# Memory cross-attention: the order of scores, transposes and value products against the query chunks

## The chip, the cores and the metric

One NeuronCore of a Trainium2 chip runs the whole program. The metric is the time of one execution on the device in microseconds; it is given as a median of several runs. All times below that have a place ("at 1289.87") are microseconds from the first instruction of one profiled execution. In the rows of the windows each busy time is followed by its instructions in brackets, and a clock of 1.00 is the full 2.4 GHz.

## The reference, cut to what matters

The program computes a long chain of layers on 256 tokens of width 1024: a gated linear attention, a differential attention, two MLPs, a mixing block with a convolution, a state-space branch and a sliding-window attention, then a cross-attention to a memory of 256 entries, and a last MLP. The change touches the cross-attention only:

```python
def memory_cross_attention(h, mem_h, w_q, w_kv, q_g, k_g, w_o):
    q = rms_norm_2((h @ w_q).reshape(b, l, XATTN_HEADS, XATTN_HEAD_DIM), q_g)   # 4 heads of 256
    kv = mem_h @ w_kv
    k = rms_norm_2(kv[..., :D_MODEL].reshape(b, m, XATTN_HEADS, XATTN_HEAD_DIM), k_g)
    v = kv[..., D_MODEL:].reshape(b, m, XATTN_HEADS, XATTN_HEAD_DIM)
    logits = jnp.einsum("bqhd,bkhd->bhqk", q, k).astype(jnp.float32) * (XATTN_HEAD_DIM ** -0.5)
    probs = jax.nn.softmax(logits, axis=-1)
    out = jnp.einsum("bhqk,bkhd->bqhd", probs.astype(v.dtype), v).reshape(b, l, D_MODEL)
    return out @ w_o
```

`h` is the residual stream after the mixing block. All of it is fp32.

## The kernel before, in words

**Chunks.** All large weights are one stream of 420 chunks of 1024 x 128, numbered in the order in which they are used. The mix output is chunks C_MIX = 332 to 339, the query projection C_XQ = 340 to 347, the attention's output projection C_XO = 348 to 355, the last MLP starts at C_M2 = 356. SyncE loads two chunks at a time (a slab, 1 MB) into a ring of four (`raw`). ScalarE (ACT) copies a chunk to an fp32r high part `w_hi` (`cut_hi`, line 1064), VectorE (DVE) subtracts and writes the bf16 rest `w_lo` (`cut_lo`, line 1692). Both run three chunks ahead (AHEAD = 3) in four slots. TensorE (PE) multiplies a chunk in 24 matmuls: 16 with `w_hi` against the high and low part of the activations (lines 425 and 426), 8 with `w_lo` (line 435). The result, 128 x 256, lies in one PSUM bank until DVE reads it out, which is called eviction here and counted by the semaphore `bank_free`. Chunks go round four banks, 0 to 3; `chunk(..., banks=2)` goes round banks 0 and 1 and waits before its first matmul for the eviction of the chunk two before it. The activations come in three forms, too (`operand` on ACT makes the high and the bf16 form, `operand_lo` on DVE the low one), and the first chunk of a group waits for them one by one.

**Order.** There is no scheduler: each engine has its own instruction order, written out by hand, and semaphores between them. An instruction that waits holds up all behind it on its engine.

**The stage of the change.** On PE the eight query chunks come first. Behind chunk 0 is a matmul for the row norm (`stats(6)`, its logarithm and exponential on ACT are `rms(6)`), and DVE needs that to evict chunk 0 (`scaled`, line 1711, multiplies by it). Two chunks are one head of the query. When both are evicted, ACT squares them (`pair_sq`, line 1543), PE sums the squares with a matmul of ones (`pair_sums`, line 923), ACT makes the reciprocal root in two steps (`pair_rstd`, lines 1547 and 1550), and DVE multiplies the head by gain and root (`pair_out`, line 2224). The pair sums 4 to 7 of the query use banks 4 and 5 in turn (`pair_sums_at`).

Then, after all chunks, come the four heads of attention, all in plain fp32 matmuls, which the trace shows as two instructions each:

- `x_scores(h)` on PE, line 1010, eight instructions, into bank 4 + h%2. The scores of head h + 1 stand before the transposes of head h. The first waits until all queries are normed.
- maximum on DVE (`x_max`, line 2318), exponential with sums on ACT (`x_exp`, line 1651), reciprocal and weights on DVE (lines 2332, 2334).
- transposes on PE (line 1023), into bank 6; copy to SBUF on ACT (line 1662).
- value products on PE (line 1032), eight instructions, into bank 7 or 3.
- ACT reads them into the operand of the output projection (`operand`, lines 1070, 1071: four casts a head), DVE makes the low part (`x_lo`, line 1705). The output chunks' first one waits for these one by one, so its last products wait for head 3.

Of the kernel before, what the change touches and what calls it, by code (L numbers as in the profile page):

```python
# [24 lines left out]
T = 256  # L25
KC = D // P
# [11 lines left out]
X_HEADS = 4  # L38
# [37 lines left out]
AHEAD = 3  # L76
# [14 lines left out]
OUT_BANKS = (7, 3)  # L91
# [26 lines left out]
def program(nc, w_d, par_d, con_d, gm_d, x_d, mem_d, band_d, out_d):  # L118
    ctx = ExitStack()
    with ctx:  # L120
# [159 lines left out]
        x_q = cut(KC, T)  # L280
# [81 lines left out]

        def pair_sums_at(k):

            return ps[:, 2 if k < X_HEADS else 4 + k % 2, 0:T]

        def tap_sums(i):

# [39 lines left out]
        def _(pe):  # L408
            mm = nc.tensor.matmul

            def chunk(c, j, X, build, banks=BANKS):

                chunk_hi(c, j, X, build, banks)
                chunk_rest(c, j, X, build, banks)
# [88 lines left out]
            def chunks(c0, n, X, build, banks=BANKS):  # L503
                for j in range(n):
                    chunk(c0 + j, c0 + j, X, build if j == 0 else None, banks)

            def stats(nu, row, tok):

                pe.wait_ge(sq_step, (2 * KC - 1) * (nu + 1))
                if nu:  # L510
                    pe.wait_ge(rstd_done, nu)
                if row:
                    last = mm(stat_rstd(), ones[:], sumsq[:], start=True, stop=True)
                if tok:
                    for t in range(NT):
                        last = mm(stat_tok()[:, t:t + 1], sumsq[:, t * P:(t + 1) * P], ones[:, 0:1], start=True, stop=True)
                last.then_inc(stat_mm, 1)
# [398 lines left out]
            def pair_sums(k):  # L916
                pe.wait_ge(xa["sq"], k + 1)
                if k >= 2:
                    pe.wait_ge(xa["r"], k - 1)
                if 0 < k < X_HEADS:  # L920
                    pe.wait_ge(xa["r"], k)
                for i in range(2):
                    last = mm(pair_sums_at(k), ones[:], x_sq[:, k % 2, i], start=i == 0, stop=i == 1)  # L923
                last.then_inc(xa["mm"], 1)
# [67 lines left out]
            chunks(C_MIX, 8, XB, XB_MIX)  # L992


            for n in range(9):
                if n < 8:
                    chunk(C_XQ + n, C_XQ + n, XA, XA_XQ if n == 0 else None)
                    if n == 0:
                        stats(6, True, False)
                if n and n % 2 == 0:  # L1000
                    pair_sums(4 + n // 2 - 1)

            def x_scores(h):
                if h == 0:
                    pe.wait_ge(xa["out"], 16)
                if h >= 2:
                    pe.wait_ge(xa["p"], h - 1)
                for t in range(NT):
                    for i in range(2):
                        last = mm(ps[:, 4 + h % 2, t * T:(t + 1) * T], x_q[:, 2 * h + i, t * P:(t + 1) * P], x_k[:, 2 * h + i],  # L1010
                                  start=i == 0, stop=i == 1)
                last.then_inc(xa["s"], 1)

            x_scores(0)
            for h in range(X_HEADS):
                if h + 1 < X_HEADS:
                    x_scores(h + 1)
                pe.wait_ge(xa["n"], h + 1)
                if h:
                    pe.wait_ge(xa["pt"], h)  # L1020
                for k in range(2):
                    for t in range(NT):
                        last = nc.tensor.transpose(ps[:, 6, k * T + t * P:k * T + (t + 1) * P], x_p[:, h % 2, t, k * P:(k + 1) * P], ident)
                last.then_inc(xa["t"], 1)
                pe.wait_ge(xa["pt"], h + 1)
                if h >= 2:
                    pe.wait_ge(XB.lo_done, KC * XB_XO + 2 * h - 2)
                    pe.wait_ge(XB.bf_done, KC * XB_XO + 2 * h - 2)
                for half in range(2):
                    f = slice(h * T + half * P, h * T + (half + 1) * P)  # L1030
                    for k in range(2):
                        last = mm(ps[:, OUT_BANKS[h % 2], half * T:(half + 1) * T], x_v[:, k, f], x_pt[:, h % 2, k], start=k == 0, stop=k == 1)  # L1032
                last.then_inc(xa["o"], 1)
            chunks(C_XO, 8, XB, XB_XO)
            mlp(C_M2, 2, XA_MLP2, C_M2 - 3, 0, XB_MLP2, 7)

# [2 lines left out]
        def _(act):  # L1039
# [13 lines left out]
            def cut_hi(c, j):  # L1053

                if isinstance(c, int) and c >= CHUNKS:
                    return
                if j % 2 == 0:
                    if isinstance(c, int):
                        act.wait_ge(slab_in[j // 2 % RING], 16 * (c // 2 // RING + 1))
                    else:  # L1060
                        act.wait_ge(slab_in[j // 2 % RING], 2 * (c - j % 8) + 16)
                if not isinstance(c, int) or c >= HI_SLOTS:
                    act.wait_ge(gemm_done, c - HI_SLOTS + 1)
                nc.scalar.copy(w_hi[:, j % HI_SLOTS].rearrange("p k n -> p (k n)"),  # L1064
                               raw[:, j // 2 % RING, j % 2]).then_inc(hi_done, 1)
# [10 lines left out]
            def rms(nu, to, to_tok=None):  # L1076

                act.wait_ge(stat_mm, nu + 1)
                if to_tok is not None:
                    A(lnt_tok[:], stat_tok(), ACT.Ln, bias=eps[:, 0:1], scale=1.0 / D)  # L1080
                done(A(lnt[:, 0], stat_rstd(), ACT.Ln, bias=eps[:, 0:1], scale=1.0 / D))
                if to_tok is not None:
                    A(to_tok[:], lnt_tok[:], ACT.Exp, scale=-0.5)
                A(to[:], lnt[:, 0], ACT.Exp, scale=-0.5).then_inc(rstd_done, 1)
# [546 lines left out]
                operand(XB, XB_MIX, n, merged[:, n])  # L1631
            residual(C_MIX, XA, XA_XQ, "norm_xattn")

            cut_hi(C_XQ + AHEAD, C_XQ + AHEAD)
            for n in range(10):
                if n < 8:
                    if n < 7:
                        cut_hi(C_XQ + n + 1 + AHEAD, C_XQ + n + 1 + AHEAD)
                    if n == 0:
                        rms(6, rstd)  # L1640
                    if n % 2:
                        pair_sq(4 + n // 2, C_XQ + n, x_q[:, n - 1:n + 1])
                if n >= 2 and n % 2 == 0:
                    pair_rstd(4 + n // 2 - 1)

            def x_exp(h):
                act.wait_ge(xa["max"], h + 1)
# [4 lines left out]
                            accum_out=x_st[:, h % 2, 2 + t:3 + t])  # L1652
                ins.then_inc(xa["p"], 1)

            x_exp(0)
            for h in range(X_HEADS):
                if h + 1 < X_HEADS:
                    x_exp(h + 1)
                act.wait_ge(xa["t"], h + 1)
                if h >= 2:  # L1660
                    act.wait_ge(xa["o"], h - 1)
                nc.scalar.copy(x_pt[:, h % 2].rearrange("p a b -> p (a b)"), ps[:, 6, :]).then_inc(xa["pt"], 1)
                act.wait_ge(xa["o"], h + 1)
                for half in range(2):
                    operand(XB, XB_XO, 2 * h + half, ps[:, OUT_BANKS[h % 2], half * T:(half + 1) * T])
            residual(C_XO, XA, XA_MLP2, "norm_mlp2")
            mlp(C_M2, 2, 7, 0, None, None, None)

# [7 lines left out]
        def _(dve):  # L1676
# [32 lines left out]
            def scaled(c, j, to, banks=BANKS):  # L1709

                TT(to, got(c, j, banks), rstd[:], ALU.mult).then_inc(bank_free, 1)
# [590 lines left out]
            residual(C_MIX, XA, XA_XQ, "norm_xattn")  # L2302


            for n in range(12):
                if n < 8:
                    c = C_XQ + n
                    cut_lo(c + AHEAD, c + AHEAD)
                    if n == 0:
                        dve.wait_ge(rstd_done, 7)  # L2310
                    scaled(c, c, x_q[:, n])
                if n >= 4 and n % 2 == 0:
                    k = n // 2 - 2
                    pair_out(4 + k, x_q[:, 2 * k:2 * k + 2], gains[:, 0:2])

            def x_max(h):
                dve.wait_ge(xa["s"], h + 1)
                V.tensor_reduce(x_st[:, h % 2, 0:2], ps[:, 4 + h % 2, :].rearrange("p (c k) -> p c k", c=2), AX.X, ALU.max,
                                negate=True).then_inc(xa["max"], 1)

            def x_lo(h):
                dve.wait_ge(XB.bf_done, KC * XB_XO + 2 * h + 2)
                for half in range(2):
                    operand_lo(XB, KC * XB_XO + 2 * h + half + 1, 2 * h + half, ps[:, OUT_BANKS[h % 2], half * T:(half + 1) * T])

            x_max(0)
            for h in range(X_HEADS):
                if h + 1 < X_HEADS:
                    x_max(h + 1)
                st = x_st[:, h % 2]  # L2330
                dve.wait_ge(xa["p"], h + 1)
                done(V.reciprocal(st[:, 4:6], st[:, 2:4]))
                for t in range(NT):
                    ins = TS(x_p[:, h % 2, t], x_p[:, h % 2, t], st[:, 4 + t:5 + t], None, ALU.mult)
                ins.then_inc(xa["n"], 1)
                if h:
                    x_lo(h - 1)
            x_lo(X_HEADS - 1)
            residual(C_XO, XA, XA_MLP2, "norm_mlp2")
            mlp(C_M2, 2, 7, XB_MLP2, None, None, None)  # L2340

# [257 lines left out]
```

## Time and profile before

| | us |
|---|---|
| time, median of 3 runs | 1522.74 (1521.49 to 1523.23) |
| span of the profiled execution, first to last instruction | 1523.5 |
| PE busy | 1400.5 (92%) |
| PE weight loads busy | 1275.7 (84%) |
| DVE busy | 1033.1 (68%) |
| ACT busy | 894.8 (59%) |
| POOL busy | 316.7 (21%) |
| mean granted TensorE clock | 0.975 of full |

The profiled execution has no time of its own beside its span, which is what the rows are measured against. Busy shares are those of the whole program. The span in 40 slices has this line for PE: `7998999999999999999777788989898799799999`; the stage of the change lies between 1264 and 1325 us, in the slices 34 and 35 (counted from 1), which carry a 9 and a 7.

### The profile page before, as it was taken

Reading aid. Unit: us, or ns where it says so; the run is one execution under the profiler, and the core shown is the slowest. Engines: PE = TensorE matmul, PEld = TensorE weight load, DVE = VectorE, ACT = ScalarE, POOL = GpSimd, SP = SyncE. Lnnn points to the kernel's source line nnn. Section 1 sums busy time; section 2 is a strip of 40 time slices with the busy share of each in tenths; the row PEclk is TensorE's granted clock in tenths of the full one; section 3 lists DMA queues with packets and bytes.
Section 4 is the critical chain, followed back from the end, with each engine's and each line's share of the span. In section 5 each row is a group of like instructions: output and inputs, shape, how many; then the busy total and the mean of one; then the engine's idle time right before and its main releaser. Section 6 shows DMA issues by size and latency. Waiting matters only on the chain. (4 is left out here: it accounts for less than half of the span.)

```text
span 1523.5 us, 29982 instructions
## 1 busy us (share of the span) xinstructions
PE 1400.5 (92%) x11466; PEld 1275.7 (84%) x11466; DVE 1033.1 (68%) x1638; ACT 894.8 (59%) x1713; POOL 316.7 (21%) x321
## 2 busy tenths in 40 slices
PE   7998999999999999999777788989898799799999
PEld 6888999988888999998777677869786598699998
DVE  6787766575678555779998556567576676375555
ACT  5456555466776544679886654544564565465443
POOL 2002211150003111349874000004000022041111
PEclk9999999999999999999999899999999899999999
DMA  7323555546634555454444233235343344055552
GB/s 313 121 103 110 194 194 193 194 165 133 205 134 148 200 194 193 152 194 143 158 142 141 85 107 111 84 111 178 130 136 137 113 167 166 32 191 194 194 194 82
DMA packets 35603, 233.72 MB, mean 153 GB/s; under 512 B 4000, under 2 KB 7072, under 8 KB 8352
## 3 DMA queue, kind: packets, MB, share of 16 engines
q1 hardware_dynamic: 31104, 223.75, 41.1%
q10 hardware_dynamic: 3216, 4.19, 1.8%
q0 software_dynamic: 1168, 4.20, 1.0%
q8 instruction: 78, 1.28, 0.3%
q14 instruction: 37, 0.30, 0.1%
HBM read 227.93 MB, written 4.19 MB: 152 GB/s over the span
## 5 line engine op out<-in xcount | busy, mean ns | idle before, releaser
L1692 DVE TENSOR_TENSOR w_lo<-raw,w_hi 128x1024 bf16<-128x1024 f32 x420 | 536.6, 1279 | 211.0 <-ACT w_hi L1064 209.9
L1064 ACT CAST w_hi<-raw 128x1024 fp32r<-128x1024 f32 x420 | 437.8, 1047 | 292.3 <-PE ps L435 139.1
L425 PE MATMUL ps<-xa_both,w_hi 128*128 128x256 f32 x1768 | 451.0, 295 | 22.8 <-ACT w_hi L1064 10.3
L426 PE MATMUL ps<-xa_both,w_hi 128*128 128x256 f32 x1768 | 427.3, 282 | 0.0
L425 PEld LDWEIGHTS ps<-xa_both,w_hi 128*128 128x128 f32 x1768 | 341.4, 193 | 31.4 <-issue 14.9
L426 PEld LDWEIGHTS ps<-xa_both,w_hi 128*128 128x128 f32 x1768 | 341.8, 193 | 0.9 <-issue 0.2
L435 PE MATMUL ps<-xa_bf,w_lo 128*128 128x256 bf16 x1768 | 233.8, 276 | 21.7 <-DVE w_lo L1692 21.6
L494 PE MATMUL ps<-xb_both,w_hi 128*128 128x256 f32 x832 | 204.7, 288 | 0.1
L435 PEld LDWEIGHTS ps<-xa_bf,w_lo 128*128 128x128 bf16 x1768 | 156.8, 99 | 49.0 <-DVE w_lo L1692 25.6
L495 PE MATMUL ps<-xb_both,w_hi 128*128 128x256 f32 x832 | 195.1, 277 | 0.0
L494 PEld LDWEIGHTS ps<-xb_both,w_hi 128*128 128x128 f32 x832 | 156.6, 188 | 1.5 <-DVE xb_both L1707 0.3
L495 PEld LDWEIGHTS ps<-xb_both,w_hi 128*128 128x128 f32 x832 | 156.6, 188 | 0.1
L2396 POOL TENSOR_TENSOR arena<-arena 128x256 f32<-128x256 f32 x96 | 69.8, 728 | 390.4 <-DVE arena L1774 390.4
L2432 POOL TENSOR_TENSOR arena<-arena 128x512 f32<-128x512 f32 x90 | 127.2, 1414 | 46.0 <-ACT arena L1398 35.5
L425 PE MATMUL ps<-xb_both,w_hi 128*128 128x256 f32 x448 | 114.2, 295 | 9.0 <-DVE xb_both L1705 4.5
L500 PE MATMUL ps<-xb_bf,w_lo 128*128 128x256 bf16 x832 | 108.9, 274 | 0.0
L426 PE MATMUL ps<-xb_both,w_hi 128*128 128x256 f32 x448 | 108.1, 282 | 0.0
L425 PEld LDWEIGHTS ps<-xb_both,w_hi 128*128 128x128 f32 x448 | 86.3, 193 | 13.9 <-issue 12.5
L426 PEld LDWEIGHTS ps<-xb_both,w_hi 128*128 128x128 f32 x448 | 86.4, 193 | 0.1
L500 PEld LDWEIGHTS ps<-xb_bf,w_lo 128*128 128x128 bf16 x832 | 73.2, 98 | 10.5
L1398 ACT ACTIVATE arena<-arena,par 128x256 f32<-128x256 f32 x180 | 77.5, 497 | 6.3 <-POOL arena L2432 6.3
L1070 ACT CAST xb_both<-arena 128x256 fp32r<-128x256 f32 x136 | 55.1, 405 | 33.7 <-POOL arena L2396 30.2
(311 smaller groups left out, 1940.2 us busy)
## 6 DMA issues: line engine op xcount, KB each, us to landing
raw<-weights SPq DMA_DIRECT2D x210, 1024.0 KB, 4.8
band<-arena ACTq DMA_DIRECT2D x1, 3072.0 KB, 35.5
arena<-band POOLq DMA_DIRECT2D x8, 256.0 KB, 3.2
arena<-gla_masks SPq DMA_DIRECT2D x1, 1088.0 KB, 15.0
H<-x_t SPq DMA_DIRECT2D x2, 512.0 KB, 4.3
arena<-mem_t POOLq DMA_DIRECT2D x1, 1024.0 KB, 5.3
arena<-band POOLq DMA_DIRECT2D x8, 128.0 KB, 2.6
out_t<-H ACTq DMA_DIRECT2D x8, 128.0 KB, 2.0
```

The costliest lines, as they stand in the source:

```text
L425: mm(ps[:, bank, 0:T], w_hi[:, s, k], X.hi[:, k], start=k == 0, stop=False)
L426: mm(ps[:, bank, 0:T], w_hi[:, s, k], X.lo[:, k], start=False, stop=False)
L435: last = mm(ps[:, bank, 0:T], w_lo[:, s, k], X.bf[:, k], start=False, stop=k == KC - 1)
L494: mm(sums(n), w_hi[:, s, i], X.hi[:, k], start=opens, stop=False)
L495: mm(sums(n), w_hi[:, s, i], X.lo[:, k], start=False, stop=False)
L500: done = mm(sums(n), w_lo[:, s, i], X.bf[:, k], start=False, stop=last and (k, n) == DOWN[j][-1] and j >= 4)
L1064: nc.scalar.copy(w_hi[:, j % HI_SLOTS].rearrange("p k n -> p (k n)"), raw[:, j // 2 % RING, j % 2]).then_inc(hi_done, 1)
L1070: nc.scalar.copy(X.hi[:, k], src).then_inc(X.hi_done, 1)
L1398: A(c_prod[:, a % PRODUCTS, i % 2], c_in[:, i, k:k + T], ACT.Copy, scale=w).then_inc(ca["prod"], 1)
L1692: TT(w_lo[:, j % HI_SLOTS].rearrange("p k n -> p (k n)"), raw[:, j // 2 % RING, j % 2], w_hi[:, j % HI_SLOTS].rearrange("p k n -> p (k n)" ...
L2396: G.tensor_tensor(m_sq[:, j % 2], m_relu[:, j % 2], m_relu[:, j % 2], ALU.mult).then_inc(sq_done, 1)
L2432: G.tensor_tensor(both, both, c_prod[:, a % PRODUCTS], ALU.add).then_inc(ca["add"], 1)
```

## The change

On PE, the four heads' steps are split into `x_scores`, `x_turn` (transposes) and `x_values`, and the loops are replaced by a written-out order in which scores(0), transposes(0), scores(1) and values(0) stand between the query chunks. ACT's and DVE's orders are written out to match. The query chunks use two banks instead of four (banks 2 and 3 are free for pair sums and values), and two waits are added: chunk 0 waits for all evictions of the mix chunks, the output chunks for all of the query chunks. The pair sums of the query use the two halves of bank 2. `x_scores(h)` waits for head h's gains instead of all. No instruction is added or removed.

```diff
--- before.py
+++ after.py
@@ -362,7 +362,7 @@
 
         def pair_sums_at(k):
 
-            return ps[:, 2 if k < X_HEADS else 4 + k % 2, 0:T]
+            return ps[:, 2, 0:T] if k < X_HEADS else ps[:, 2, k % 2 * T:(k % 2 + 1) * T]
 
         def tap_sums(i):
 
@@ -992,17 +992,11 @@
             chunks(C_MIX, 8, XB, XB_MIX)
 
 
-            for n in range(9):
-                if n < 8:
-                    chunk(C_XQ + n, C_XQ + n, XA, XA_XQ if n == 0 else None)
-                    if n == 0:
-                        stats(6, True, False)
-                if n and n % 2 == 0:
-                    pair_sums(4 + n // 2 - 1)
+            def xq_chunk(n):
+                chunk(C_XQ + n, C_XQ + n, XA, XA_XQ if n == 0 else None, banks=2)
 
             def x_scores(h):
-                if h == 0:
-                    pe.wait_ge(xa["out"], 16)
+                pe.wait_ge(xa["out"], 2 * X_HEADS + 2 * h + 2)
                 if h >= 2:
                     pe.wait_ge(xa["p"], h - 1)
                 for t in range(NT):
@@ -1011,10 +1005,7 @@
                                   start=i == 0, stop=i == 1)
                 last.then_inc(xa["s"], 1)
 
-            x_scores(0)
-            for h in range(X_HEADS):
-                if h + 1 < X_HEADS:
-                    x_scores(h + 1)
+            def x_turn(h):
                 pe.wait_ge(xa["n"], h + 1)
                 if h:
                     pe.wait_ge(xa["pt"], h)
@@ -1022,6 +1013,8 @@
                     for t in range(NT):
                         last = nc.tensor.transpose(ps[:, 6, k * T + t * P:k * T + (t + 1) * P], x_p[:, h % 2, t, k * P:(k + 1) * P], ident)
                 last.then_inc(xa["t"], 1)
+
+            def x_values(h):
                 pe.wait_ge(xa["pt"], h + 1)
                 if h >= 2:
                     pe.wait_ge(XB.lo_done, KC * XB_XO + 2 * h - 2)
@@ -1031,6 +1024,34 @@
                     for k in range(2):
                         last = mm(ps[:, OUT_BANKS[h % 2], half * T:(half + 1) * T], x_v[:, k, f], x_pt[:, h % 2, k], start=k == 0, stop=k == 1)
                 last.then_inc(xa["o"], 1)
+
+            pe.wait_ge(bank_free, C_XQ)
+            xq_chunk(0)
+            stats(6, True, False)
+            xq_chunk(1)
+            xq_chunk(2)
+            pair_sums(4)
+            xq_chunk(3)
+            x_scores(0)
+            xq_chunk(4)
+            pair_sums(5)
+            xq_chunk(5)
+            x_turn(0)
+            x_scores(1)
+            xq_chunk(6)
+            x_values(0)
+            pair_sums(6)
+            xq_chunk(7)
+            x_turn(1)
+            x_scores(2)
+            pair_sums(7)
+            x_values(1)
+            x_scores(3)
+            x_turn(2)
+            x_values(2)
+            x_turn(3)
+            x_values(3)
+            pe.wait_ge(bank_free, C_XO)
             chunks(C_XO, 8, XB, XB_XO)
             mlp(C_M2, 2, XA_MLP2, C_M2 - 3, 0, XB_MLP2, 7)
 
@@ -1631,17 +1652,8 @@
                 operand(XB, XB_MIX, n, merged[:, n])
             residual(C_MIX, XA, XA_XQ, "norm_xattn")
 
-            cut_hi(C_XQ + AHEAD, C_XQ + AHEAD)
-            for n in range(10):
-                if n < 8:
-                    if n < 7:
-                        cut_hi(C_XQ + n + 1 + AHEAD, C_XQ + n + 1 + AHEAD)
-                    if n == 0:
-                        rms(6, rstd)
-                    if n % 2:
-                        pair_sq(4 + n // 2, C_XQ + n, x_q[:, n - 1:n + 1])
-                if n >= 2 and n % 2 == 0:
-                    pair_rstd(4 + n // 2 - 1)
+            def q_sq(k):
+                pair_sq(4 + k, C_XQ + 2 * k + 1, x_q[:, 2 * k:2 * k + 2])
 
             def x_exp(h):
                 act.wait_ge(xa["max"], h + 1)
@@ -1652,17 +1664,49 @@
                             accum_out=x_st[:, h % 2, 2 + t:3 + t])
                 ins.then_inc(xa["p"], 1)
 
-            x_exp(0)
-            for h in range(X_HEADS):
-                if h + 1 < X_HEADS:
-                    x_exp(h + 1)
+            def x_turned(h):
                 act.wait_ge(xa["t"], h + 1)
                 if h >= 2:
                     act.wait_ge(xa["o"], h - 1)
                 nc.scalar.copy(x_pt[:, h % 2].rearrange("p a b -> p (a b)"), ps[:, 6, :]).then_inc(xa["pt"], 1)
+
+            def x_operand(h):
                 act.wait_ge(xa["o"], h + 1)
                 for half in range(2):
                     operand(XB, XB_XO, 2 * h + half, ps[:, OUT_BANKS[h % 2], half * T:(half + 1) * T])
+
+            def ahead(n):
+                cut_hi(C_XQ + n + AHEAD, C_XQ + n + AHEAD)
+
+            ahead(0)
+            ahead(1)
+            rms(6, rstd)
+            ahead(2)
+            q_sq(0)
+            ahead(3)
+            pair_rstd(4)
+            ahead(4)
+            q_sq(1)
+            x_exp(0)
+            ahead(5)
+            pair_rstd(5)
+            q_sq(2)
+            ahead(6)
+            x_turned(0)
+            x_exp(1)
+            ahead(7)
+            pair_rstd(6)
+            x_operand(0)
+            q_sq(3)
+            x_turned(1)
+            pair_rstd(7)
+            x_exp(2)
+            x_operand(1)
+            x_turned(2)
+            x_exp(3)
+            x_operand(2)
+            x_turned(3)
+            x_operand(3)
             residual(C_XO, XA, XA_MLP2, "norm_mlp2")
             mlp(C_M2, 2, 7, 0, None, None, None)
 
@@ -2302,40 +2346,58 @@
             residual(C_MIX, XA, XA_XQ, "norm_xattn")
 
 
-            for n in range(12):
-                if n < 8:
-                    c = C_XQ + n
-                    cut_lo(c + AHEAD, c + AHEAD)
-                    if n == 0:
-                        dve.wait_ge(rstd_done, 7)
-                    scaled(c, c, x_q[:, n])
-                if n >= 4 and n % 2 == 0:
-                    k = n // 2 - 2
-                    pair_out(4 + k, x_q[:, 2 * k:2 * k + 2], gains[:, 0:2])
+            def xq_chunk(n):
+                c = C_XQ + n
+                cut_lo(c + AHEAD, c + AHEAD)
+                if n == 0:
+                    dve.wait_ge(rstd_done, 7)
+                scaled(c, c, x_q[:, n], 2)
+
+            def q_out(k):
+                pair_out(4 + k, x_q[:, 2 * k:2 * k + 2], gains[:, 0:2])
 
             def x_max(h):
                 dve.wait_ge(xa["s"], h + 1)
                 V.tensor_reduce(x_st[:, h % 2, 0:2], ps[:, 4 + h % 2, :].rearrange("p (c k) -> p c k", c=2), AX.X, ALU.max,
                                 negate=True).then_inc(xa["max"], 1)
 
-            def x_lo(h):
-                dve.wait_ge(XB.bf_done, KC * XB_XO + 2 * h + 2)
-                for half in range(2):
-                    operand_lo(XB, KC * XB_XO + 2 * h + half + 1, 2 * h + half, ps[:, OUT_BANKS[h % 2], half * T:(half + 1) * T])
-
-            x_max(0)
-            for h in range(X_HEADS):
-                if h + 1 < X_HEADS:
-                    x_max(h + 1)
+            def x_weights(h):
                 st = x_st[:, h % 2]
                 dve.wait_ge(xa["p"], h + 1)
                 done(V.reciprocal(st[:, 4:6], st[:, 2:4]))
                 for t in range(NT):
                     ins = TS(x_p[:, h % 2, t], x_p[:, h % 2, t], st[:, 4 + t:5 + t], None, ALU.mult)
                 ins.then_inc(xa["n"], 1)
-                if h:
-                    x_lo(h - 1)
-            x_lo(X_HEADS - 1)
+
+            def x_lo(h):
+                dve.wait_ge(XB.bf_done, KC * XB_XO + 2 * h + 2)
+                for half in range(2):
+                    operand_lo(XB, KC * XB_XO + 2 * h + half + 1, 2 * h + half, ps[:, OUT_BANKS[h % 2], half * T:(half + 1) * T])
+
+            xq_chunk(0)
+            xq_chunk(1)
+            xq_chunk(2)
+            q_out(0)
+            xq_chunk(3)
+            x_max(0)
+            xq_chunk(4)
+            x_weights(0)
+            q_out(1)
+            xq_chunk(5)
+            x_max(1)
+            xq_chunk(6)
+            x_weights(1)
+            q_out(2)
+            xq_chunk(7)
+            x_lo(0)
+            x_max(2)
+            q_out(3)
+            x_weights(2)
+            x_lo(1)
+            x_max(3)
+            x_weights(3)
+            x_lo(2)
+            x_lo(3)
             residual(C_XO, XA, XA_MLP2, "norm_mlp2")
             mlp(C_M2, 2, 7, XB_MLP2, None, None, None)
 
```

## Rows read from the trace of the kernel before

**Rows 1.** Windows: length; busy PE, PEld, DVE, ACT, POOL; clock, DMA, GB/s. Chunks, attention.

```profile
1268.10:1289.90 21.80, 21.75 (x181) 20.38 (x179) 12.95 (x20) 11.82 (x18) 0.00 (x0) 1.00 0.54 186
1289.90:1324.40 34.50, 23.25 (x96) 17.98 (x96) 10.08 (x29) 13.09 (x40) 0.00 (x0) 0.90 0.01 5
```

**Rows 2.** Chain of waits, 1225 to 1345: start, length, what (xN are merged).

```profile
1264.69 0.44 DVE H L1729
...
1266.32 0.38 PE ps L425
...
1270.91 0.12 PE ps L425
...
1273.63 0.86 PE ps L923 x4
...
1288.97 0.90 PE ps L435 x8
...
1291.03 1.15 PE ps L923 x4
...
1293.16 0.89 DVE arena L2224 x2
1294.09 5.42 PE ps L1010 x16
...
1304.33 1.74 PE ps L1010 x8
...
1307.56 0.67 PE ps L1023 x4
...
1308.90 1.99 PE ps L1032 x8
...
1315.46 3.52 PE ps L1032 x8
...
1320.74 2.01 PE ps L1032 x8
...
1324.48 0.38 PE ps L425
```

**Rows 3.** Timeline of PE: the first query chunk's first product, and the fourteenth.

```profile
1264.41 0.37 PE L425 MATMUL ps<-xa_both,w_hi 128*128 128x256 f32 x1
...
1265.98 0.28 PE L426 MATMUL ps<-xa_both,w_hi 128*128 128x256 f32 x1
```

**Rows 4.** Timelines of DVE and ACT: an eviction, exponentials(0), operand(0), first and last instruction.

```profile
1269.71 0.42 DVE L1711 TENSOR_TENSOR arena<-ps,rstd 128x256 f32<-128x256 f32 x1 [1.45 <-ACT rstd L1084]
...
1298.13 0.47 ACT L1651 ACTIVATE arena<-ps,arena 128x256 f32<-128x256 f32 x1 [5.00 <-DVE arena L2318]
...
1298.95 0.20 ACT L1651 ACTIVATION_READ_ACCUMULATOR arena<-ps,arena 128x1 f32 x1
...
1304.37 0.37 ACT L1070 CAST xb_both<-ps 128x256 fp32r<-128x256 f32 x1 [2.08 <-PE ps L1032]
...
1305.17 0.40 ACT L1071 CAST xb_bf<-ps 128x256 bf16<-128x256 f32 x1
```

**Rows 5.** Groups by line and form, 1240 to 1330: count, busy, mean ns, idle before.

```profile
L1692 DVE TENSOR_TENSOR w_lo<-raw,w_hi 128x1024 bf16<-128x1024 f32 x19 | 23.8, 1251 | 7.0 <-ACT w_hi L1064 7.0
...
L1064 ACT CAST w_hi<-raw 128x1024 fp32r<-128x1024 f32 x20 | 21.0, 1052 | 18.2 <-PE ps L435 18.2
...
L2318 DVE TENSOR_REDUCE arena<-ps 128x2 f32<-128x512 f32 x4 | 2.8, 692 | 14.4 <-PE ps L1010 14.4
...
L1543 ACT ACTIVATE arena<-arena 128x512 f32<-128x512 f32 x4 | 2.5, 628 | 2.1 <-DVE arena L1711 2.1
```

**Rows 6.** Windows with the granted clock: sliding-window stage, its end, the first scores.

```profile
1180.00:1190.00 10.00, 10.00 (x87) 8.38 (x86) 5.62 (x14) 5.90 (x15) 0.72 (x1) 1.00 0.28 110
1210.00:1220.00 10.00, 4.50 (x22) 3.73 (x23) 2.86 (x10) 8.36 (x21) 0.00 (x0) 0.50 0.00 0
1296.00:1298.00 2.00, 2.00 (x6) 1.57 (x5) 0.60 (x1) 0.00 (x0) 0.00 (x0) 0.50 0.00 0
```

## The prediction

> **What bounds the kernel now.** I read the windows first. While the eight query chunks run, TensorE is busy 21.75 of 21.8 us at full clock; in the 34.5 us behind them, the attention itself, it is busy 23.25 us at a mean clock of 0.90, and DVE and ACT are below 40%: nobody is full, the engines hand one head to each other [rows 1]. Then the chain of waits, which shows what stands in that tail: the last query chunk ends at 1289.87, the pair sum waits for the square and runs to 1292.18, scores(0) and scores(1) start at 1294.09, and the output chunk's last operand is multiplied at 1324.48 [rows 2]. So 34.6 us, of which the reader should see three things. Handovers between engines: from the pair sum's end to the scores 1.91 us (logarithm, exponential, two gains); from the end of scores(2) (1306.07) to the transposes 1.49 (maximum and weights); from the transposes' end (1308.23) to the values 0.67 (the PSUM copy); from the last values' end (1322.75) to the output chunk 1.73 [rows 2]. Low clock: two heads' scores took 5.42 us where one took 1.74, and values(2) took 3.52 where values(1) took 1.99 [rows 2]; around the former the granted clock was 0.50, which is 1.2 GHz [rows 6]. And honest matmul time: at full clock 0.86 for the pair sum and per head 1.74 + 0.67 + about 1.75 to 1.99.
>
> **The change, part by part.** I lay the new order out on the times of before. All sums are against the profiled span of 1523.5 us; time around the span isn't shown, and the median of the runs, 1522.74, is 0.8 us lower, so I take the difference off the median.
>
> Unit prices on PE at full clock: chunk 2.72 (1270.91 to 1273.63), pair sum 0.86, scores 1.74, transposes 0.67, values 1.74 where they follow other work (eight instructions of the scores' kind) and 1.99 after a wait [rows 2]. Elsewhere: two exponentials with their reads 1.02 and four operand casts 1.20, first start to last end [rows 4]; maximum 0.69, hi cut 1.05, lo cut 1.25, square 0.63 [rows 5]; so the weights are 1.49 less 0.69, 0.8.
>
> *The new wait in front of chunk 0* (all mix chunks evicted). The last eviction ends at 1265.13 [rows 2]; chunk 0 had begun at 1264.41, but stalled before its last operand: 1265.98 to 1266.32 where instructions are 0.12 apart, 0.22 too much [rows 3, 2]. So it starts 0.72 later and gets back 0.2 at most. Bounds 0.5 to 0.72 (a gain is excluded, it waits for more); I take 0.55, as the products that come late then run without the stall. Behind this wait on PE stands everything, and nothing else hides it.
>
> *Two banks.* Chunk n needs the eviction of n-2. The tightest is chunk 2: eviction 0 ended at 1270.13 [rows 4], now 1270.7, and chunk 2 wants to start at 1271.46. Later ones have over 3 us: eviction 3 about 1278.8 for chunk 5 at 1283.1; eviction 5 about 1286.8 for chunk 7 at 1293.5. Cost nothing; if DVE were 0.8 us later at chunk 2, it would show at once.
>
> *The PE order.* Ends, each the sum of the prices: chunk 2 1274.18, pair sum 4 1275.04, chunk 3 1277.76, scores(0) 1279.50, chunk 4 1282.22, pair sum 5 1283.08, chunk 5 1285.80, transposes(0) 1286.47, scores(1) 1288.21, chunk 6 1290.93, values(0) 1292.67, pair sum 6 1293.53, chunk 7 1296.25, transposes(1) 1296.92, scores(2) 1298.66, pair sum 7 1299.52, values(1) 1301.26. What each needs is there before: scores(0) needs the gains of pair 0: ACT first cuts a hi part (to 1275.3), so they end near 1277.2, 0.6 before. Transposes(0): exponentials end near 1281.3, but the weights stand in DVE behind eviction 4 (1282.7), so 1283.5 against 1285.80. Scores(1): gains at 1285.0 against 1286.47. Values(0): ACT's queue holds square 2 behind eviction 5 (to 1287.4), a hi cut (1288.5), the copy (1289.1), against 1290.93. Transposes(1): weights about 1292.2 against 1296.25. Scores(2): gains 1295.4 against 1296.92. Pair sum 7: chunk 7 ends at 1296.25, but DVE stands in the lo cut begun at 1295.4, to 1296.65; eviction 1297.1, square 1297.7, against 1298.66. Values(1): copy 1298.3 against 1299.52. The narrowest margins are 0.6 and 0.9.
>
> *What stays open behind.* Scores(3) need 1.91 after pair sum 7: start 1301.43, end 1303.17. Exponentials(2) follow that root on ACT (1301.5) and the weights end at 1302.4, so transposes(2) run at once, to 1303.84; the copy costs 0.67, values(2) run 1304.51 to 1306.50. ACT meanwhile does exponentials(3) (1305.5), DVE the weights (1306.3): transposes(3) 1306.50 to 1307.17. Now ACT has operand(2) queued ahead of the copy: 1306.5 + 1.2 + 0.6 = 1308.40; values(3) end at 1310.39, and the tail of 1.73 stays: 1312.12. That place was 1324.48: **12.4 us less**. The lateness that remains is 0.17, 0.67, 1.23 and 1.73, in the order of scores(3), values(2), values(3) and the output chunk.
>
> *Moved work that costs nothing.* The eight hi and lo cuts keep their order among themselves, three chunks ahead; the lo cut of output chunk 2 ends at 1296.65, 14 us before it is used. The weight transfers follow these cuts. The DMA stood nearly still in the tail of before, 5 GB/s [rows 1], with its ring full; it reaches the output chunks full in both orders. The pair sums' new place (halves of bank 2 in place of banks 4 and 5) changes no duration; it frees 4 and 5 for scores. The stronger wait on the gains asks for 10, 12, 14, 16 in turn, met as above. The wait for all query evictions before the output chunks is met 13 us before.
>
> *The clock.* In the new order PE has no gap over 0.2 us until 1303.84, so the fall that cost scores(0) and (1) 5.42 - 3.48 = 1.94 should go. At the end there are gaps of 0.67 and 1.23 in 5 us, much like the old cycle of one head, in one of three of which the clock fell. My 12.4 has none in it; one fall costs from nothing to 1.9. Two-bank chunks with small matmuls between them exist in before, in the sliding-window stage: ten microseconds of it show PE busy throughout and the clock at 1.00, while a stretch where PE was busy 4.5 of 10 us shows 0.50 [rows 6].
> The Trainium skill ("TensorE: Matmul & The Clock Gate", section "A second HAM failure mode: psum-queue depth-cycling") speaks against this change: it says that cycling through PSUM banks makes TensorE idle briefly and often enough to lose the clock. By it the time would be that of the third rival below; by the row above, the sum stands.
>
> **Rivals.** *Uncovered pieces.* The handovers of the interleaved pieces aren't hidden, because DVE and ACT run in order and each small step stands behind a cut or an eviction. If scores(0), transposes(0), scores(1) and values(0) pay in full what they paid in the tail, 1.91 + 1.49 + 1.91 + 0.67 = 6.0 us come back: gain 6.4, time 1516.3. For it: margins of 0.6 to 0.9 us; against: they are positive, and DVE was busy only 12.95 of the 21.8 us of the query chunks [rows 1].
> *It moves nothing.* The output chunks can't start earlier because their weights aren't cut or loaded, so the tail is merely waited out: 1522.7. For it: nothing but that the SP queue is tied to the cuts; against: the 5 GB/s in the tail, that is, the ring was waiting and not wanted.
> *Slower: the clock falls inside the query chunks.* One mechanism: mixing plain fp32 pieces with two-bank chunks makes PE pause, and it runs at 1.2 GHz. From scores(0) to values(3) there are 4 x 2.72 + 4 x (1.74 + 0.67 + 1.74) + 3 x 0.86 = 30.1 us of matmul time at full clock, which would each double. It decides for slower where more than 12.4 of these 30.1 us run at half rate; with 16 of them, 1526. For it: the 0.50 of rows 6; against: no pauses in my order before 1303.84, and the 1.00 beside it. It is this result that the skill's section named above would give.
>
> **Chances.** Forecast (one clock fall at the end or none) 0.82; uncovered pieces 0.10; moves nothing 0.04; slower 0.04. The time is the likeliest's: 1522.74 - 12.4 = 1510.4. Its own range: 0.5 us less if chunk 0 costs nothing and up to 1.2 less if the copy before values(3) is early; more by 1.9 for a clock fall and by some tenths at each of the seventeen joints between pieces, which I price at zero, about 1.5; with the 0.9 us by which single runs of before differ: 1508.3 to 1514.8. What that leaves out is most of the rivals, 0.18. Faster by over 0.2%, 3 us, which is about what a measurement of this kernel can tell from no change: forecast and uncovered pieces, with a little of the second, 0.93; same 0.03; slower 0.04.
>
> **What would show it.** Right: chunk 0 begins right behind the last eviction of the mix chunks, near 1265.2; scores(0), transposes(0), scores(1) and values(0) follow chunk products with no idle time; from the last query chunk's end to the last operand's product of the first output chunk 15.9 us in place of 34.6; waits of PE only before scores(3), values(2), values(3); the clock at 1.00 until 1303. Wrong: a PE wait on an eviction (two banks too few); idle time before scores(0) or pair sum 7; a clock below 1 in the query chunks; or the same lead at 1312 and a loss of it in the output chunks or the MLP.

## The result, and the profile after

The changed kernel takes 1511.0 us, median of 4 runs (1509.56 to 1514.88), against 1522.99 us before (4 runs): ratio 0.992, 95% interval 0.9905 to 0.9934, that is 12.2 us less, 10.0 to 14.5. A second set of 6 runs beside 17 of before gave 0.993 (0.9918 to 0.9942), 10.7 us less. The forecast was 1510.4, 12.4 us less. Two single executions among the runs below were in a slow state (2318.2 us of "one head between the chunks", 6377.3 us of "before, clock held up") and the ratios leave them out; they move the medians below by at most 0.2 us.

The profiled execution took 1511.23 us with a span of 1509.4; the 1.8 us between lie outside first and last instruction. The two spans differ by 14.1 us, not 12, and 1.1 of it was there before the stage begins: the eviction of the last mix chunk starts at 1263.57 where it started at 1264.69 [rows 2], though the code up to it is the same. Below I therefore measure each profile **from that eviction's start to its last instruction**: 258.8 us before, 245.8 after, 13.0 less. A repeated profile of the changed kernel gave 245.8 again. The difference is complete where the first output chunk's last operand is multiplied: from the eviction to there it is 59.79 us before and 46.82 after, 12.97 less, and nothing of it is lost in the output chunks and the MLP behind.

First comes the chain of waits after the change, from the stage's start to the output chunk's last operand; it answers to [rows 2]. Line 1004 is scores, 1014 transposes, 1025 values, 923 pair sums, 513 the row norm's matmul behind chunk 0, and 1773 the eviction of a mix chunk.

```profile
1263.57 0.43 DVE H L1773
1264.05 0.38 PE ps L425
...
1267.04 0.43 PE ps L513 x2
...
1276.56 1.73 PE ps L1004 x8
...
1284.60 0.44 PE ps L1014 x4
1285.04 1.73 PE ps L1004 x8
...
1289.49 1.73 PE ps L1025 x8
...
1294.81 0.44 PE ps L1014 x4
1295.25 1.73 PE ps L1004 x8
1296.98 0.88 PE ps L923 x4
...
1299.77 1.99 PE ps L1004 x8
1301.76 0.45 PE ps L1014 x4
...
1302.88 2.01 PE ps L1025 x8
...
1306.65 2.01 PE ps L1025 x8
...
1310.39 0.38 PE ps L425
```

What to see: up to 1297.86 the chain is PE alone, one piece beginning where the other ends. The eviction, the exponential and the weights of heads 0 and 1 have left the chain. From the last query chunk's end (1294.81) to the last operand's product it is 15.6 us, where it was 34.6. The tail is so much shorter because scores(0), transposes(0), scores(1) and values(0) now stand before it; what the whole stage gains is the 13.0.

Next come the windows of the two parts, query chunks and what is behind them, against [rows 1] (length, then busy PE, weight loads, DVE, ACT, POOL, then clock, DMA share, GB/s):

```profile
1263.60:1294.80 31.20, 30.75 (x236) 28.87 (x237) 18.42 (x32) 17.65 (x34) 1.78 (x3) 1.00 0.43 152
1294.80:1310.40 15.60, 13.04 (x70) 10.70 (x67) 7.11 (x20) 8.91 (x27) 0.00 (x0) 1.00 0.00 1
```

The clock is 1.00 in both, also where two-bank chunks and plain fp32 pieces alternate. The same view over the whole stage, from the eviction's start to the last operand's product, first before and then after:

```profile
1264.69:1324.48 59.79, 48.36 (x302) 41.34 (x300) 25.57 (x51) 27.13 (x61) 1.82 (x3) 0.94 0.23 80
1263.57:1310.39 46.82, 43.79 (x302) 39.55 (x302) 25.55 (x51) 26.55 (x61) 1.81 (x3) 1.00 0.29 102
```

PE does the same 302 instructions. It was idle for 11.4 us and is idle for 3.0 now, so 8.4 of the 13.0 us are idle time that is gone. The other 4.6 are the same instructions taking less time, by the clock and because they no longer follow a wait. PE's waits in the whole stage (who waited for whom, us in total, times, longest):

```profile
PE ps L1025 <- ACT arena L1671: 2.0, 2, 1.3
PE ps L425 <- DVE H L1773: 0.5, 1, 0.5
PE ps L425 <- DVE xb_both L1749: 0.3, 1, 0.3
PE ps L1004 <- DVE arena L2268: 0.2, 1, 0.2
```

These are the ones that were forecast: values(2) and (3) for their copies, chunk 0 for the added wait, the output chunk for the last operand, scores(3) for its gains. PE doesn't wait for any query eviction. The wait for the last operand is only 0.3 us, though 1.73 us lie between the values' end and that product: for most of that time PE multiplies the operands of heads 0 to 2.

### The profile page after: what moved, and what is told of

It is laid out like the page before. It is cut to its first block and busy times, and to the rows that moved or that the text cites. A ratio compares the mean times of both kernels' runs of the same rounds, so it can differ in the third digit from the quotient of the medians.

```text
span 1509.4 us, 29986 instructions
## 1 busy us (share of the span) xinstructions
PE 1396.9 (93%) x11466; PEld 1275.1 (84%) x11466; DVE 1032.9 (68%) x1638; ACT 893.9 (59%) x1713; POOL 316.4 (21%) x321
## 5 line engine op out<-in xcount | busy, mean ns | idle before, releaser
L425 PEld LDWEIGHTS ps<-xb_both,w_hi 128*128 128x128 f32 x448 | 86.4, 193 | 13.8 <-issue 12.4
## 6 DMA issues: line engine op xcount, KB each, us to landing
arena<-gla_masks SPq DMA_DIRECT2D x1, 1088.0 KB, 14.9
```

Source lines behind the costliest of these rows:

```text
L425: mm(ps[:, bank, 0:T], w_hi[:, s, k], X.hi[:, k], start=k == 0, stop=False)
```

## The experiments

The prediction left a question that its sum doesn't need: PE has something to do in every handover now, but must that be the query chunks? "From the stage" is the measure defined above, from one profile of each kernel, and its difference is taken to the kernel before (258.8) and rounded afterwards.

| kernel | median us | ratio to before, interval | from the stage, difference |
|---|---|---|---|
| changed kernel, again | 1512.23 | 0.9930 (0.9918 to 0.9942) | 245.8, -13.0 |
| all heads behind the chunks, dense | 1512.15 | 0.9931 (0.9919 to 0.9943) | 245.1, -13.8 |
| one head between the chunks | 1514.74 | 0.9936 (0.9920 to 0.9953) | 246.7, -12.1 |
| before, clock held up | 1523.08 | 0.9992 (0.9980 to 1.0003) | 255.6, -3.2 |
| before, bank part alone | 1524.75 | 0.9997 (0.9984 to 1.0011) | 260.8, +2.0 |
| dense, coarse wait | 1519.61 | 0.9971 (0.9962 to 0.9980) | 251.4, -7.4 |
| changed, no added wait | 1510.36 | 0.9908 (0.9890 to 0.9927) | 245.5, -13.4 |
| changed, gains late | 1514.30 | 0.9933 (0.9917 to 0.9950) | 247.8, -11.0 |
| changed, gaps filled | 1508.21 | 0.9894 (0.9879 to 0.9910) | 243.1, -15.7 |
| dense behind, gaps filled | 1508.65 | 0.9899 (0.9883 to 0.9915) | 243.0, -15.8 |

**Is it the cover of the chunks?** This kernel puts all of the attention behind the query chunks. The two banks, the two added waits and the finer waits of the change stay. TensorE's order, from chunk 2 on, is this (an abridged diff to the changed kernel; ACT's and DVE's orders follow it):

```diff
+ c2 pair_sums(4) c3 c4 pair_sums(5) c5 c6 pair_sums(6) c7        # c = query chunk
+ x_scores(0) x_scores(1) pair_sums(7) x_turn(0) x_scores(2) x_values(0) x_turn(1)
+ x_scores(3) x_values(1) x_turn(2) x_values(2) x_turn(3) x_values(3)
  ...
- x_operand(2); x_turned(3)       # on ACT
+ x_turned(3); x_operand(2)
```

> Nothing of the attention stands between the query chunks; all of it comes behind them, but in a dense order and with the finer waits of the change (scores(h) waits for its own head's gains; two banks and the added waits are kept). Theory A (the gain is the cover: pieces hidden beside the chunks): the tail is long again, at most the clock falls go, 3 to 5 us gained over before, so 1518 to 1520. Theory B (PE only needs something to do in every handover, and pieces of other heads serve as well as chunks; the sum of PE work is the same): laid out by the unit prices, 20.2 us from the last query chunk to the output chunk's last operand, gain over before 13 us, 1510, about 1 less than the changed kernel, because the last copy stands before operand(2) here.

The chain of this kernel from the last mix eviction, and below it the window of the tail:

```profile
1260.94 0.43 DVE H L1773
...
1286.56 1.74 PE ps L1004 x8
...
1290.97 0.66 PE ps L1014 x4
1291.63 1.73 PE ps L1004 x8
1293.36 1.73 PE ps L1025 x8
1295.09 0.44 PE ps L1014 x4
1295.52 1.73 PE ps L1004 x8
1297.25 1.73 PE ps L1025 x8
...
1306.94 0.39 PE ps L425
```

```profile
1286.60:1306.90 20.30, 18.56 (x96) 15.47 (x94) 10.40 (x29) 12.60 (x40) 0.00 (x0) 1.00 0.03 10
```

Theory A falls and B holds: with nothing between the chunks the tail takes 20.4 us (1286.56 to 1306.94; 20.2 were laid out), and PE is busy 18.56 of 20.3. The whole is 0.8 us shorter than the changed kernel in the profile and the same in the runs. Scores(1) and pair sum 7 cover head 0's softmax, scores(2) its copy, and so on.

The step in between puts only head 0 among the chunks (ACT's and DVE's orders follow again):

```diff
- xq_chunk(5) x_turn(0) x_scores(1) xq_chunk(6) x_values(0) pair_sums(6) xq_chunk(7) x_turn(1) x_scores(2) pair_sums(7) x_values(1)
+ xq_chunk(5) x_turn(0) xq_chunk(6) x_values(0) pair_sums(6) xq_chunk(7) x_scores(1) pair_sums(7) x_scores(2) x_turn(1) x_values(1)
```

> Only head 0 (scores, transposes, values) stands between the query chunks; scores(1) and all behind it come after the last chunk. Theory A (cover by chunks, in proportion to the work placed there: 3.9 of 5.9 us): two thirds of the gain, 8 us, 1515. Theory B (dense order): laid out by unit prices the last operand comes 0.3 us later than in the changed kernel, so 1511.3.

It is 0.9 us behind the changed kernel in the profile, where theory B had 0.3 and A 4. The runs (9.8 us less than before, 7.3 to 12.2) don't tell the two theories apart: A had about 8 less, B about 12. So this one rests on the profile. Its chain from scores(1) on: head 1's softmax is just covered (pair sum 7 and scores(2) take 2.6 of the 2.7 us from 1295.92 to the transposes), but its copy is bare: 0.66 us with nothing beside it on PE.

```profile
1294.18 1.74 PE ps L1004 x8
...
1298.60 0.67 PE ps L1014 x4
1299.29 0.59 ACT arena L1671
1299.93 2.00 PE ps L1025 x8
```

**How much is clock?** Unused matmuls fill PE's pauses in the kernel before:

```diff
+ def fill(n): n times mm(ps[:, 0, 0:T], ones[:], x_k[:, 0], start=True, stop=True)
+ fill(2) before pair_sums(7); fill(3) before x_scores(0)
+ fill(2) before each of the first three transposes; fill(1) before each x_values
```

> The kernel before, with unused matmuls of ones by a key tile into free bank 0 wherever TensorE waited in the tail (2 before pair sum 7, 3 before scores(0), 2 before each of the first three transposes, 1 before each value product), 0.43 us each at full clock. It tells what of the gain is clock. Theory: the clock stays at 1.00, scores(0) and (1) take 3.5 instead of 5.4 and values(2) 2.0 instead of 3.5: 3.4 us less, 1519.5, and no more, the handovers stay. If the clock were the bigger part of the gain, 1514 or less. If the fill itself gets into the path, up to 1 us is lost of the 3.4.

Two lines of its chain, scores(0) with (1) and values(2), and its window of the tail:

```profile
1295.00 3.73 PE ps L1018 x16
...
1314.68 2.01 PE ps L1044 x8
```

```profile
1290.80:1322.00 31.20, 26.51 (x126) 20.59 (x124) 9.97 (x28) 12.96 (x40) 0.00 (x0) 1.00 0.01 5
```

The clock stays at 1.00, scores(0) and (1) take 3.73 instead of 5.42 and values(2) 2.01 instead of 3.52 [rows 2]: 3.2 us, where 3.4 were expected. The handovers stay as long as they were. So in these profiles about a quarter of the 13.0 is clock. Of the rest, 8.4 is idle time and about 1.4 is the lower price of pieces that no longer follow a wait. The runs say 1.2 us with an interval from 3.0 to -0.5, so the profile's 3.2 lies just outside it. The profiled execution of before had a mean clock of 0.975, and the 17 executions of it beside this kernel had 0.975 to 0.979, 0.977 on average. So it was one of those that lost most to the clock, and on average the share is probably smaller; in which stage the others lost theirs, no run shows. It may also be why the runs have 12.2 and 10.7 us less for the changed kernel where the profile has 13.0.

**The bank part alone**, in the kernel before:

```diff
- return ps[:, 2 if k < X_HEADS else 4 + k % 2, 0:T]
+ return ps[:, 2, 0:T] if k < X_HEADS else ps[:, 2, k % 2 * T:(k % 2 + 1) * T]
+ pe.wait_ge(bank_free, C_XQ)      # before query chunk 0; and C_XO before output chunk 0
+ ...banks=2 in chunk() and scaled()
```

> The kernel before, with only the bank part of the change: query chunks in two banks, pair sums in bank 2, the two added waits. Theory: chunk 0 begins behind the last mix eviction and the rest follows 0.45 us later (what the changed kernel's trace shows, 3.47 against 3.02 us from that eviction's start to chunk 0's end), nothing else: 1523.4, same. Rival (two banks let DVE's evictions hold up PE): several waits of PE on evictions and 2 us or more.

```profile
1264.68 0.43 DVE H L1731
...
1268.20 0.43 PE ps L513 x2
...
1294.53 6.79 PE ps L1011 x16
...
1304.14 3.67 PE ps L1033 x8
...
1318.94 2.01 PE ps L1033 x8
```

In the kernel before, the same matmul behind chunk 0 (line 513) stands here in the chain:

```profile
1267.71 0.43 PE ps L513 x2
```

So chunk 0 ends 3.52 us behind the eviction's start instead of 3.02, which is 0.5 later, and 0.45 are left of that at the last query chunk's end. PE waits for no eviction among the query chunks after it. The other 1.5 of the +2.0 are the clock, which fell at other places than in the profile of before (it is 0.54 in the windows of both slow pieces): scores(0) and (1) 6.79 instead of 5.42, values(0) 3.67 instead of 1.99, values(2) 2.01 instead of 3.52. The runs show no difference.

The counterpart takes that wait out of the changed kernel (chunk 0's own wait suffices for its bank):

```diff
-            pe.wait_ge(bank_free, C_XQ)
             xq_chunk(0)
```

> The changed kernel without the wait for all mix evictions before query chunk 0 (chunk 0's own wait then asks for the eviction of mix chunk 6). Theory: chunk 0 starts 0.7 us earlier, stalls 0.2 before its last operand, all behind it 0.45 us earlier; 0.45 less than the changed kernel, 1510.5. Rival: the eviction was no limit, 0.

```profile
1264.34 0.43 DVE H L1772
...
1267.36 0.43 PE ps L513 x2
...
1310.71 0.40 PE ps L425
```

Chunk 0 ends at 3.02 again, and from the eviction to the last operand it is 46.37 instead of 46.82: 0.45, as expected. The runs are too coarse for it: the intervals of this kernel and the changed one overlap.

**The finer wait.** This is the dense tail with the scores waiting for all gains, as in the kernel before. That wait forces pair sum 7 ahead of scores(0), and the gains of head 3 ahead of the first maximum on DVE:

```diff
-                pe.wait_ge(xa["out"], 2 * X_HEADS + 2 * h + 2)
+                pe.wait_ge(xa["out"], 4 * X_HEADS)
- x_scores(0) x_scores(1) pair_sums(7) x_turn(0)
+ pair_sums(7) x_scores(0) x_scores(1) x_turn(0)
```

> The dense tail behind all query chunks, but scores wait for all gains again, as in the kernel before, and pair sum 7 stands ahead of scores(0). It parts the gain of the dense tail between the finer wait and the rest. Theory: from the last chunk to the first transposes it was 4.4 us with the finer wait and becomes 4.2 + 1.7 + 2.7 = 8.6, so 4.2 us worse than the dense tail, about 1516, up to 1.9 more if the clock falls in the pause. Rival (the finer wait is of no weight, the order is all): less than 1 us worse.

Its chain from the last mix eviction, and the windows at the pause and behind it:

```profile
1268.68 0.44 DVE H L1773
...
1295.47 1.15 PE ps L923 x4
...
1298.53 6.78 PE ps L1004 x16
1305.31 0.44 PE ps L1014 x4
```

```profile
1296.00:1299.00 3.00, 1.07 (x4) 0.66 (x3) 0.88 (x2) 0.89 (x2) 0.00 (x0) 0.82 0.00 0
1299.00:1301.00 2.00, 2.00 (x6) 1.55 (x6) 0.00 (x0) 0.00 (x0) 0.00 (x0) 0.50 0.00 0
```

It is 6.4 us worse than the dense tail. That is more than the 4.2 expected and 0.3 more than the 6.1 with the clock's fall that I had allowed for. The pauses of 1.2 and 1.9 us around pair sum 7 are back, and behind them both scores run at about half clock (0.50, which is 1.2 GHz, in the window shown) for 6.78 us, where the pair took 3.73 behind a wait at full clock. So about 3 of the 6.4 is clock, and the rest is nearly all pause. The runs agree (0.9971 against 0.9931, 6 us). So about half of the dense tail's gain hangs on one semaphore value and the order that it allows: head 0 need not wait for head 3's gains. The dense order alone keeps the other half (7.4 us). The finer wait alone, in the order of before, wasn't run.

**The margins.** Three unused DVE operations between a head's root and its gains:

```diff
             def q_out(k, late=0):
+                dve.wait_ge(xa["r"], 4 + k + 1)
+                for _ in range(late):
+                    done(TT(hn_sqb[:], H[:, 6:8], H[:, 6:8], ALU.max))
...
-            q_out(0)
+            q_out(0, 3)
```

> The changed kernel, with three unused DVE operations (128x512, about 0.75 us each, 2.3 in all) between the root of pair 0 and its gains. The gains of head 0 ended 0.7 us before scores(0) wanted them. Theory: a margin, paid in full beyond: scores(0) starts 1.6 us late, everything behind it shifts by that, 1.6 more than the changed kernel, 1512.6. Rival (later margins take it up): no change.

```profile
1275.12 0.70 DVE hn_sqb L2381
...
1277.30 0.89 DVE arena L2268 x2
1278.24 1.99 PE ps L1004 x8
```

2.2 us are put in and 1.9 come out at the end (247.8 against 245.8; 1.6 were expected): scores(0) now follow the gains directly and nothing later takes it up. They start 1.5 us later than in the changed kernel, so the margin was 0.7, about what the prediction had (0.6). Beyond it the price is full, and the piece that now follows a wait costs 1.99 instead of 1.73 besides. The runs can't tell this kernel from the changed one.

**A better version.** Two kernels put the first output chunks' early products (from the operands of heads 0 to 2) into the gaps before values(2), values(3) and the last operand, and drop the added wait. One builds on the changed kernel's order, with the last copy ahead of operand(2); the other on the dense tail, with two operands and their low-part products in each of the first two gaps. The diff is the first one's, abridged:

```diff
+ xo_hi(0, range(3))               # output chunk 0, high part, operands 0 to 2
  x_values(2); x_turn(3)
+ xo_hi(0, range(3, 4)); xo_rest(0, range(4))
  x_values(3)
+ xo_hi(0, range(4, 6)); xo_rest(0, range(4, 6)); xo_hi(1, range(4))
+ xo_hi(0, range(6, 8)); xo_rest(0, range(6, 8)); xo_hi(1, range(4, 8)); xo_rest(1, range(8))
```

> The changed kernel without the added wait, with the last copy before operand(2) on ACT, and with the first output chunk's early products put into PE's gaps before values(2) and values(3), and four operands of output chunk 1 into the last one. Theory: 0.45 from chunk 0, 0.65 from the copy, 0.67 + 0.92 from products that no longer stand behind the last operand: 2.7 less than the changed kernel, 1508.3. Rival: the gaps are handovers, and what is put there delays the values by as much: 1 us or less.

> The dense tail behind all query chunks, without the wait added before query chunk 0, and with the first output chunks' early products in PE's gaps before values(2), values(3) and the last operand. Nothing of the attention lies between query chunks. Theory B (dense order is what counts): 0.45 and 1.6 less than the dense tail alone, the same as the filled version of the changed kernel within 0.3 us: ratio to before 0.989. Theory A: at least 3 us worse than that one.

Both came out as laid out, 2.7 and 2.9 us less than the changed kernel from the stage on (243.1 and 243.0). By the runs they take 16.2 and 15.4 us less than before, and each one's interval contains the other's ratio. The window of the first one's tail shows PE with 0.3 us idle of 14.9:

```profile
1292.70:1307.60 14.90, 14.59 (x83) 12.17 (x81) 7.08 (x20) 8.94 (x27) 0.00 (x0) 1.00 0.01 2
```

What bounds this stage now is TensorE's own work.

## Why the prediction was right, point by point

**What bounds the tail.** This was right. It was read as handovers, low clock and honest matmul time. The parts of the 13.0 are shown: 3.2 us of clock by the kernel with held clock, 8.4 of idle time by the windows, and 1.4 that the same pieces take less when they don't follow a wait. The dense tail shows that PE's work there takes 18.6 us. One reading went too far: the 1.73 us before the output chunk's last operand are not all a handover, PE is idle in only 0.3 of them.

**The added wait.** I took 0.55. The two kernels that isolate it measured 0.45 and 0.45 to 0.50, at or just under my lower bound of 0.5.

**Two banks.** They cost nothing, as said: the trace of the changed kernel has no wait on a query eviction. The Trainium skill ("TensorE: Matmul & The Clock Gate", section "A second HAM failure mode: psum-queue depth-cycling") reports a kernel that lost clock by cycling through banks, because TensorE was briefly idle again and again between its groups of matmuls. Here TensorE was idle for only 0.45 of the 31.2 us with two-bank chunks, and the granted clock was 1.00, so the trace doesn't confirm the rule for this case and doesn't contradict its reason.

**The unit prices.** Transposes behind other work take 0.44, not 0.67, which is the price after a wait. That is 0.23 too much at each of the three places where they count (transposes(3) are hidden behind ACT). Scores(3), which follow a wait, take 1.99, not 1.74, so 0.25 too little. That both ways of following have a price of their own I had applied to the values only. Values(3) start 1.76 us after values(2) end, and the sum had 1.90. Of these 0.14, 0.1 is a slip of addition: 1306.5 + 1.2 + 0.6 is 1308.30 and not 1308.40. Together with 0.1 at chunk 0 this makes 0.7, and some hundredths come back at the values, which leaves the 0.6 between 12.4 forecast and 13.0 measured in the profile.

**The lateness left.** The forecast was 0.17, 0.67, 1.23 and 1.73; measured were 0.2, 0.7, 1.3 and 1.73 (1308.66 to 1310.39). The third is a little longer than forecast because transposes(3) are over sooner.

**The clock at the end.** I gave one fall a place in the range and none in the forecast. None came in the two profiles of the changed kernel.

**The range, and luck.** The range's terms add up to 1507.8 to 1514.7, where 1508.3 to 1514.8 is on record; the measured 1511.0 lies in both. That the median came within 0.6 us of the forecast is partly luck. Two sets of runs gave 12.2 and 10.7 us less, the profile gave 13.0, and single executions of the changed kernel lie 5 us apart, which is much more than the 0.9 that I had allowed for.

**The first rival** (pieces not covered) didn't occur, but its condition was the true weak point: once a margin is used up, everything beyond it is paid in full. **The second and third** didn't occur: the lead of 13.0 at the last operand is still 13.0 at the end, and the clock is 1.00 in the whole stage.

**What the prediction did not see.** Its sum names PE's work and gaps only, which is why it holds. But it doesn't say whether the query chunks are needed as cover, and a reader could take the interleaving for the cause. It isn't: the same gain comes with all four heads behind the chunks. What gives it there is that a piece of another head stands in nearly every handover, and that a head waits for its own gains.

## What to carry to other kernels

Where engines hand one item to each other in turn, lay the bounding engine's pieces end to end, with another item's piece in each handover; which piece it is hardly mattered here as long as its inputs were ready, so try first the order that interleaves no stages. (The dense tail kept the two banks and the added waits; whether it can do without them wasn't run.) Look at each wait for "all of them" and ask whether the first item needs the last: in the dense tail that was about half of the gain, part of it because the clock fell in the pause and stayed low for the work behind it. Price every piece twice, after other work and after a wait: the scores took 1.73 and 1.99 us, the transposes 0.44 and 0.67.

## What the runs showed of the hardware

The same code ahead of the stage ended at times from 1260.94 to 1268.68 (the last mix eviction's start) in twelve profiles, nearly 8 us apart, which is more than several of the differences asked about. The measure from a common instruction on gave the same 245.8 us in both profiles of the changed kernel. Between the dense tail and its coarse-wait version, the two furthest apart, the difference grows along the way: it is 3.0 us at the first product of line 598 (55.7 against 58.7) and 7.0 at the first transpose of line 975 (1077.3 against 1084.3). What causes it stays open.

The clock fell behind short pauses in the three profiled kernels that have the old pauses around pair sum 7 and no fill. It did so at scores(0) and values(2) in [rows 2], at scores(0) and values(0) in the bank kernel, and at scores(0) in the coarse-wait kernel, where its mean was already 0.84 over the pause of 1.9 us before them. Scores(0) and (1) together took 5.42, 6.79 and 6.78 us, where the kernel with held clock took 3.73. Pauses of 0.7 and 1.3 us with 2 us of work between them, in the changed kernel, had no such fall behind them.
